# Another dealing of the modulation slabs over the first layer's projections, and another place for their requests

## The chip, the cores and the metric

The kernel runs on one core of a Trainium2 chip. The metric is the device time of one execution in microseconds. TensorE does the matrix products, VectorE (DVE) and ScalarE (ACT) the elementwise work, GpSimd (POOL) some set-up and a few transfers; SyncE (SP) asks for nearly all transfers from HBM, in one queue.

## The reference

A decoder of two layers on 256 tokens of width 2048, in float32. Cut to what matters:

```python
cs = silu(c)                                   # one vector of 2048
for l in range(2):
    mod = cs @ ada_w[l] + ada_b[l]             # six vectors of 2048
    sh_a, sc_a, g_a, sh_m, sc_m, g_m = split(mod, 6)
    h = x * (1 + sc_a) + sh_a
    if l == 0:
        y = gla_mixer(h, w_in, ...)            # q, k, v, r = h @ w_in; gated linear attention in 4 chunks;
                                               # o = rms_norm(o) * silu(r); o @ w_out
    else:
        k, v = split((x * (1 + sc_k) + sh_k) @ w_kv)   # sh_k, sc_k = cs @ kv_ada_w + kv_ada_b
        y = stick_breaking(h @ w_q, k, v) @ w_out
    x = layer_norm(alpha * x + (1 + g_a) * y)
    h = x * (1 + sc_m) + sh_m
    x = layer_norm(alpha * x + (1 + g_m) * (relu(h @ w1 + b1) ** 2 @ w2 + b2))
```

## The kernel before

**Tiles.** The weights of the large products come in tiles of 128 x 1024 float32 (0.52 MB), 768 in all, in a fixed order of stages: `lead` (k and q of layer 0), `gv` (v, 32 tiles), `gr` (r, 32), `go` (the output projection of layer 0, 32), `u0`, `d0` (its MLP, 128 each), then layer 1. A loop body is 16 tiles (`BODY`). Each tile goes through a ring of four buffers (`RING`): SP asks for it into `raw`; ScalarE rounds it to the upper half `w_hi` (L439); VectorE subtracts to get the lower half `w_lo` (L873); TensorE multiplies the tokens' two halves by `w_hi` (L1330, L1331) and the upper one by `w_lo` (L1334), four times each. `stripe_tile` and `wide` do this in the first layer. SP may ask for tile t once VectorE has done tile t-4, ScalarE may round it once TensorE has used tile t-4.

**Slabs.** The vectors `mod` are made beside that by VectorE. A slab is 128 x 2048 float32 (1.05 MB) of the transposed modulation weights; one `scalar_tensor_tensor` (L878, in `mod_tile`) multiplies it by `cs` and sums along the row, which gives 128 elements of `mod`. There are 224 slabs, 16 to a vector. The first 32 (the shift and scale of the first product) go through eight buffers in `lead`. The other 192 share the two buffers of `mod_w`; SP may ask for a slab once the slab two before it is done:

```python
def load_mod(a, slot, first=False):
    if not first:
        sp.wait_ge(mod_done, a - 1)
    sp.dma_start(mod_w[:, slot, :], mods[bass.ds(a, 1), :, :]...)
```

In this text slabs are counted from the first of these 192 (0, 1, ...). Slabs 0 and 1 are asked for and done at the end of `lead`.

**The order.** `SCHEDULE` says for each body how many slabs are dealt to it, and `MOD_AT` behind which tiles of a body they lie for each such number. VectorE works in `body` tile by tile: the lower half, the slabs dealt to that tile, then what else hangs on the tile as a hook. SP's `body` goes the same way: it asks for tile j and then for the slabs dealt to position j, and each request waits in the queue for its own release. `MODS_DONE` (VectorE) and `MODS_LOADED` (SP) override `MOD_AT` for single bodies; before, they do so for `gv`'s first body and for `go`'s second.

**Around the change.** In `gv` VectorE has more to do than halves and slabs: the gates' logarithm (L1099), their running sums (L1105, L1114), and the keys and queries with their decays (L1126 to L1144). The gates' product is TensorE's hook behind tile 1 of `gv` (L1578), the scores' product (80 small matmuls, L1589) the one behind tile 25; ScalarE copies the scores (L670) as a hook behind tile 28, VectorE masks them behind tile 30. In `gr` TensorE has the four heads' output (L1603), in `gr` and `go` the turning of o (L1464). The slabs of `gv` make the gate `g_a0`, which is read in `gr`; those up to `go`'s second body make `sh_m0` and `sc_m0`, which are read at the end of `go` (`make_coef`).

Of the kernel before, what the change touches and what calls it, by code (L numbers as in the profile page):

```python
# [35 lines left out]
T0 = {}  # L36
_at = 0
for _n, _s in _sizes:
# [14 lines left out]

MOD_AT = {12: (0, 1, 3, 4, 5, 7, 8, 9, 11, 12, 13, 15), 10: (1, 2, 4, 5, 7, 8, 10, 12, 13, 15), 8: tuple(range(1, 16, 2)), 6: (1, 4, 6, 9, 12, 14), 4: (0, 2, 5, 9), 2: (10, 14), 0: ()}

SCHEDULE = [("gv", 0, 1, 8), ("gv", 16, 1, 10), ("gr", 0, 1, 12), ("gr", 16, 1, 8), ("go", 0, 1, 8), ("go", 16, 1, 2), ("u0", 0, 1, 0), ("u0", 16, 7, 8),
            ("d0", 0, 4, 6), ("d0", 64, 1, 2), ("d0", 80, 2, 6), ("d0", 112, 1, 0), ("aq", 0, 1, 2), ("aq", 16, 1, 6), ("ak", 0, 2, 4),
            ("av", 0, 1, 4), ("av", 16, 1, 6), ("ao", 0, 1, 8), ("ao", 16, 1, 0), ("u1", 0, 1, 0), ("u1", 16, 4, 4), ("u1", 80, 10, 0), ("d1", 112, 1, 0)]
PLAN = {}
_a = LEAD  # L60
for _n, _off, _bodies, _per in SCHEDULE:
    for _b in range(_bodies):
# [40 lines left out]
def unsplit_before(t):  # L103

    return N_LEAD + early_before(t)
# [6 lines left out]
def build_kernel(nc, tiles, mods, c_t, x_rows, mod_b, ln_t, b1_t, w_gl, wgu, normg_t, ln_rows, b2_rows, out):  # L112
# [3 lines left out]
    with ctx:  # L116
# [136 lines left out]
            return (rows_buf, turned_buf)[tok][:, pr * SEQ:(pr + 1) * SEQ]  # L253

        GO_MODS = {6: (0,), 9: (1,)}
        MODS_DONE = {T0["gv"]: {1: (2,), 3: (3,), 4: (4,), 5: (5,), 10: (6,), 15: (7,)}, T0["go"] + 16: GO_MODS}
        MODS_LOADED = {T0["gv"]: {3: (2, 3), 4: (4,), 5: (5,), 10: (6,), 15: (7,)}, T0["go"] + 16: GO_MODS}

        def mod_positions(per_body):
            return {j: (i,) for i, j in enumerate(MOD_AT[per_body])}  # L260
# [14 lines left out]
        def _(sp):  # L275
# [11 lines left out]
# [3 lines that stand above are left out]
                sp.dma_start(mod_w[:, slot, :], mods[bass.ds(a, 1), :, :].rearrange("a p n -> p (a n)"))\  # L290
                  .then_inc(mod_loaded[slot], 16)
# [16 lines left out]
            def body(t, a, per_body, at=None, skipped=0, early=False, ahead=None, from_lead=False):  # L308
                at = at or mod_positions(per_body)
                for j in range(BODY):  # L310
                    if not early or j >= EARLY:
                        load_tile(t + j, j % RING, skipped=skipped, unsplit=from_lead and j < RING)
                    if ahead is not None and j in EARLY_LOAD:
                        load_early(ahead, EARLY_LOAD.index(j))
                    for i in at.get(j, ()):
                        load_mod(a + i, i % 2)
# [24 lines left out]
            for i in range(2):  # L341
                sp.wait_ge(mod_done, LEAD - LEAD_BUFS + i + 1)
                load_mod(LEAD + i, i, first=True)
            for name, off, bodies, per in SCHEDULE:
                t = T0[name] + off
# [3 lines left out]
                if bodies == 1:  # L349
                    body(t, PLAN[t][0], per, MODS_LOADED.get(t), skipped=unsplit_before(t), early=t in EARLY_AT, from_lead=t == N_LEAD,  # L350
                         ahead=EARLY_AT.index(t + BODY) if t + BODY in EARLY_AT else None)
# [508 lines left out]
        def _(dve):  # L860
# [32 lines left out]
            def body(t, a, lap, per, hooks, early=False, at=None):  # L893
                at = at or mod_positions(per)
                for j in range(BODY):
                    if not early or j >= EARLY:
                        split_tile(t + j, j % RING, ring_used=t if early and j < EARLY + RING else None)
                    for i in at.get(j, ()):
                        mod_tile(a + i, mod_w[:, i % 2, :], mod_loaded[i % 2], lap + i // 2 + 1)
                    for f in hooks.get(j, ()):  # L900
                        f()

            def run(t, hooks=None):
                a, per = PLAN[t]
                body(t, a, (a - LEAD) // 2, per, {j: H.get(t + j, []) for j in range(BODY)} if hooks is None else hooks, t in EARLY_AT,
                     MODS_DONE.get(t))

# [907 lines left out]
```

## Time and profile before

| | |
|---|---|
| time, three runs | 2262.27, 2263.2, 2265.02 us (median 2263.2) |
| the profiled execution | 2265.58 us, its span 2263.9 us |
| TensorE busy (matmul) | 2231.3 us, 99% of the span, granted clock 0.997 |
| VectorE busy | 1723.9 us, 76% |
| ScalarE busy | 1136.3 us, 50% |
| read from HBM | 655.22 MB, 290 GB/s over the span |

The span runs from the first to the last instruction; times of day in the rows count from its start. Busy shares are averages over stages with different limits: `lead` lasts to about 144 us, `gv` to 252, `gr` to 352, `go` to 432. TensorE's matmuls overlap in the records (one of 512 columns is listed with 0.39 us and the next starts 0.23 us later), so its own progress is read from the starts of rows.

### The profile page before, as it was taken

The numbers are of one execution on the slowest core, as the hardware profiler recorded it, in microseconds if no ns is written. First come the engines' busy times: TensorE is split into PE (matmuls) and PEld (weight loads), VectorE is DVE, ScalarE is ACT, GpSimd is POOL, SyncE is SP. The second block draws the span as 40 slices with busy tenths as digits, with TensorE's granted clock in tenths as the row PEclk, the third lists the DMA queues.
The fourth block names the chain that finished last, engine by engine and source line by source line (L and its number), as shares of the span: only waits on it lengthen the run. The fifth ranks groups of instructions, "written<-read, shape, count | busy, mean of one in ns | idle before, by whom it ended". The sixth has DMA issues, their size and how long they took to land.

```text
span 2263.9 us, 32088 instructions
## 1 busy us (share of the span) xinstructions
PE 2231.3 (99%) x10940; PEld 1870.6 (83%) x10940; DVE 1723.9 (76%) x1706; ACT 1136.3 (50%) x1408; POOL 19.0 (1%) x41
## 2 busy tenths in 40 slices
PE   8999999999999999999999999999999999999998
PEld 6786788788888888888888888888888888888886
DVE  6689889988888888898777867888766455556656
ACT  2144455565555554444555555545555555444443
POOL 1000000000000000000000000000000000000000
PEclk9999999999999999999999999999999999999999
DMA  9998999679999999969768766784877555755563
GB/s 393 417 375 316 359 385 383 228 288 375 375 383 376 380 366 351 341 241 355 283 224 325 270 237 237 313 313 144 305 287 267 186 193 203 253 194 193 191 208 125
DMA packets 146474, 658.60 MB, mean 291 GB/s; under 512 B 16496, under 2 KB 16816, under 8 KB 115792
## 3 DMA queue, kind: packets, MB, share of 16 engines
q1 hardware_dynamic: 144000, 642.05, 75.8%
q0 software_dynamic: 2384, 15.37, 1.7%
q8 instruction: 54, 0.88, 0.2%
q14 instruction: 36, 0.29, 0.0%
HBM read 655.22 MB, written 2.13 MB: 290 GB/s over the span
## 4 chain that ended last, share of the span: by engine, by line
PE 84%; DMA 7%; DVE 6%; issue 2%; ACT 1%; SPq 1%; DVEq 0%; ACTq 0%
PE ps L1432 20%; PE ps L1330 16%; PE ps L1334 16%; PE ps L1331 16%; PE ps L1434 10%; DMA R<-in_mods 3%; DMA mod_w<-in_mods 2%; DMA raw<-in_tiles 2%; DVE mod_w L878 1%; DVE w_lo L873 1%; DVE X L956 1%; DVE stats L958 1%; DVE S L953 1%; PE ps L1534 0%; PE ps L1532 0%
## 5 line engine op out<-in xcount | busy, mean ns | idle before, releaser
L873 DVE TENSOR_TENSOR w_lo<-raw,w_hi 128x1024 fp32r<-128x1024 f32 x720 | 876.9, 1222 | 447.1 <-ACT w_hi L439 443.0
L439 ACT ACTIVATE w_hi<-raw 128x1024 fp32r<-128x1024 f32 x720 | 760.0, 1059 | 833.3 <-PE ps L1334 365.7
L1330 PE MATMUL ps<-w_hi,h_both 128*128 128x512 f32 x1872 | 735.8, 393 | 3.3 <-ACT w_hi L439 3.3
L1331 PE MATMUL ps<-w_hi,h_both 128*128 128x512 f32 x1872 | 729.1, 389 | 0.0
L1432 PE MATMUL ps<-h_both,w_hi 128*128 128x512 f32 x1920 | 666.3, 394 | 0.0
L1434 PE MATMUL ps<-h_both,w_lo 128*128 128x256 f32 x1920 | 532.1, 277 | 0.0
L1334 PE MATMUL ps<-w_lo,h_both 128*128 128x512 f32 x1872 | 506.9, 390 | 2.1 <-DVE w_lo L873 1.9
L878 DVE SCALAR_TENSOR_TENSOR mod_w<-mod_w,cs 128x2048 f32<-128x2048 f32 x200 | 456.9, 2285 | 30.7 <-DMA mod_w<-in_mods 22.2
L1432 PEld LDWEIGHTS ps<-h_both,w_hi 128*128 128x128 f32 x1920 | 360.0, 188 | 83.8
L1330 PEld LDWEIGHTS ps<-w_hi,h_both 128*128 128x128 f32 x1872 | 351.6, 188 | 78.9 <-ACT w_hi L439 3.7
L1334 PEld LDWEIGHTS ps<-w_lo,h_both 128*128 128x128 f32 x1872 | 350.6, 188 | 79.2 <-DVE w_lo L873 6.2
L1331 PEld LDWEIGHTS ps<-w_hi,h_both 128*128 128x128 f32 x1872 | 351.6, 188 | 72.2 <-issue 1.0
L1434 PEld LDWEIGHTS ps<-h_both,w_lo 128*128 128x128 f32 x1920 | 360.4, 188 | 0.1
L1210 DVE TENSOR_TENSOR h_both<-R,h_both 128x512 fp32r<-128x512 f32 x128 | 87.5, 684 | 2.9 <-ACT h_both L763 2.9
L763 ACT ACTIVATE h_both<-R 128x512 fp32r (+1 forms) x128 | 78.6, 614 | 0.0
L1344 PE MATMUL ps<-R,raw 128*128 128x256 f32 x256 | 56.7, 381 | 2.8 <-ACT R L624 1.4
L1344 PE MATMUL ps<-R,odd_raw 128*128 128x256 f32 x256 | 57.0, 381 | 2.2 <-ACT R L624 2.2
L1344 PEld LDWEIGHTS ps<-R,raw 128*128 128x128 f32 x256 | 48.1, 190 | 11.1 <-ACT R L624 3.0
L1344 PEld LDWEIGHTS ps<-R,odd_raw 128*128 128x128 f32 x256 | 48.1, 190 | 10.9 <-ACT R L624 4.6
L624 ACT ACTIVATE R<-R,coef 128x256 f32<-128x256 f32 x16 | 9.6, 600 | 93.2 <-DVE coef L1079 93.2
L878 DVE SCALAR_TENSOR_TENSOR R<-R,cs 128x2048 f32<-128x2048 f32 x16 | 36.7, 2292 | 19.1 <-DMA R<-in_mods 19.1
L499 ACT ACTIVATE S<-ps,b1t 128x256 f32<-128x256 f32 x120 | 46.6, 471 | 0.0
(195 smaller groups left out, 1037.6 us busy)
## 6 DMA issues: line engine op xcount, KB each, us to landing
raw<-in_tiles SPq DMA_DIRECT2D x736, 512.0 KB, 4.8
mod_w<-in_mods SPq DMA_DIRECT2D x200, 1024.0 KB, 7.1
R<-in_mods SPq DMA_DIRECT2D x16, 1024.0 KB, 21.9
odd_raw<-in_tiles SPq DMA_DIRECT2D x16, 512.0 KB, 20.3
R<-in_tiles SPq DMA_DIRECT2D x16, 512.0 KB, 6.3
R<-in_ln_rows POOLq DMA_DIRECT2D x6, 1024.0 KB, 8.3
G<-in_mods SPq DMA_DIRECT2D x4, 1024.0 KB, 22.0
S<-in_mods SPq DMA_DIRECT2D x4, 1024.0 KB, 24.0
```

Of the source, the lines that this page charges most:

```text
L439: nc.scalar.activation(w_hi[:, slot, :], raw[:, slot, :], ACT.Copy).then_inc(hi_ready, 1)
L499: ins = nc.scalar.activation(turned_buf[:, blk * SEQ:(blk + 1) * SEQ], ps[:, 4 * par + blk, SEQ:2 * SEQ], ACT.Identity, bias=b1t[:, bass.d ...
L763: nc.scalar.activation(h_hi[:, slot:slot + 2, :], R[:, bass.ds(kt * SEQ, 2 * SEQ)].rearrange("p (a t) -> p a t", a=2), ACT.Copy).then_inc( ...
L873: nc.vector.tensor_tensor(w_lo[:, slot, :], raw[:, slot, :], w_hi[:, slot, :].bitcast(F32), ALU.subtract)\
L878: nc.vector.scalar_tensor_tensor(buf, buf, 1.0, cs[:], ALU.mult, ALU.mult, accum_out=mod_t[:, bass.ds(a, 1)]).then_inc(mod_done, 1)
L1210: nc.vector.tensor_tensor(h_lo[:, slot:slot + 2, :], R[:, bass.ds(kt * SEQ, 2 * SEQ)].rearrange("p (a t) -> p a t", a=2), h_hi[:, slot:slo ...
L1330: mm(dst, h_hi[:, kt, toks], w_hi[:, slot, c], start=start, stop=False, skip_group_check=more)
L1331: return mm(dst, h_lo[:, kt, toks], w_hi[:, slot, c], start=False, stop=False, skip_group_check=more)
L1334: return mm(dst, h_hi[:, kt, tok * P:(tok + 1) * P], w_lo[:, slot, c], start=False, stop=stop, skip_group_check=more)
L1344: last = mm(ps[:, 2 * (2 * half + k) + blk // 2, (blk % 2) * SEQ:(blk % 2 + 1) * SEQ], w[:, k * SW + blk * P:k * SW + (blk + 1) * P], xT[: ...
L1432: mm(ps[:, bank, :], w_hi[:, j % RING, c], h_both[:, kt, :, :].rearrange("p a t -> p (a t)"), start=kt == 0, stop=False, skip_group_check= ...
L1434: last = mm(ps[:, bank, 0:SEQ], w_lo[:, j % RING, c], h_hi[:, kt, :], start=False, stop=kt == KT - 1, skip_group_check=True)
```

## The change

The number of slabs dealt to `gv`'s two bodies becomes 6 and 12 instead of 8 and 10; `gr` keeps 12 and 8. The order on VectorE is written out for both bodies of `gv` (`MODS_DONE`), and the places of SP's requests for both bodies of `gv` and of `gr` (`MODS_LOADED`). A request then stands at the position four tiles behind the one at which VectorE does the slab two before. So the requests for the last two slabs of `gv` stand in `gr` (entries -2 and -1). From `go` on nothing is changed.

```diff
-SCHEDULE = [("gv", 0, 1, 8), ("gv", 16, 1, 10), ("gr", 0, 1, 12), ("gr", 16, 1, 8), ("go", 0, 1, 8), ("go", 16, 1, 2), ("u0", 0, 1, 0), ("u0", 16, 7, 8),
+SCHEDULE = [("gv", 0, 1, 6), ("gv", 16, 1, 12), ("gr", 0, 1, 12), ("gr", 16, 1, 8), ("go", 0, 1, 8), ("go", 16, 1, 2), ("u0", 0, 1, 0), ("u0", 16, 7, 8),
...
         GO_MODS = {6: (0,), 9: (1,)}
-        MODS_DONE = {T0["gv"]: {1: (2,), 3: (3,), 4: (4,), 5: (5,), 10: (6,), 15: (7,)}, T0["go"] + 16: GO_MODS}
-        MODS_LOADED = {T0["gv"]: {3: (2, 3), 4: (4,), 5: (5,), 10: (6,), 15: (7,)}, T0["go"] + 16: GO_MODS}
+        MODS_DONE = {T0["gv"]: {1: (2,), 3: (3,), 4: (4,), 10: (5,)},
+                     T0["gv"] + 16: {2: (0,), 4: (1,), 7: (2,), 8: (3,), 9: (4,), 10: (5, 6), 11: (7,), 12: (8,), 13: (9,), 14: (10,), 15: (11,)},
+                     T0["go"] + 16: GO_MODS}
+        MODS_LOADED = {T0["gv"]: {3: (2, 3), 5: (4,), 7: (5,), 8: (6,), 14: (7,)},
+                       T0["gv"] + 16: {6: (2,), 8: (3,), 11: (4,), 12: (5,), 13: (6,), 14: (7, 8), 15: (9,)},
+                       T0["gr"]: {0: (-2,), 1: (-1,), 2: (0,), 3: (1,), 4: (2,), 5: (3,), 7: (4,), 8: (5,), 9: (6,), 11: (7,), 12: (8,), 13: (9,), 15: (10,)},
+                       T0["gr"] + 16: {0: (-1,), 1: (0,), 3: (1,), 5: (2,), 7: (3,), 9: (4,), 11: (5,), 13: (6,), 15: (7,)},
+                       T0["go"] + 16: GO_MODS}
```

## Rows read from the trace of the kernel before

**Rows 1.** The page: TensorE's busy time, share and instructions.

```profile
PE 2231.3 (99%) x10940; PEld 1870.6 (83%) x10940; DVE 1723.9 (76%) x1706; ACT 1136.3 (50%) x1408; POOL 19.0 (1%) x41
```

**Rows 2.** Busy time by stretch, from `gv` on; last three columns clock, DMA share, GB/s.

```profile
144.00:206.00 62.00, 59.74 (x263) 47.41 (x261) 57.79 (x62) 32.37 (x30) 1.97 (x2) 1.00 0.79 302
206.00:248.00 42.00, 39.14 (x206) 31.20 (x205) 34.95 (x34) 14.12 (x14) 0.00 (x0) 1.00 0.87 337
248.00:306.00 58.00, 58.00 (x236) 43.86 (x235) 46.45 (x43) 32.56 (x53) 0.51 (x1) 1.00 0.99 385
306.00:352.00 46.00, 46.00 (x214) 38.08 (x213) 41.30 (x38) 23.25 (x31) 0.56 (x1) 1.00 0.99 377
352.00:398.00 46.00, 46.00 (x210) 38.03 (x210) 40.84 (x39) 24.07 (x30) 1.05 (x2) 1.00 1.00 397
432.00:2263.90 1831.90, 1819.25 (x9095) 1536.17 (x9093) 1374.15 (x1341) 957.86 (x1183) 7.37 (x14) 1.00 0.74 272
```

**Rows 3.** Timeline of TensorE: lower-half products of tiles 0, 2, 3, 25, 26, 34, 64.

```profile
146.47 1.07 PE L1334 MATMUL ps<-w_lo,h_both 128*128 128x512 f32 x4
...
152.89 1.07 PE L1334 MATMUL ps<-w_lo,h_both 128*128 128x512 f32 x4
155.61 1.07 PE L1334 MATMUL ps<-w_lo,h_both 128*128 128x512 f32 x4
...
223.86 1.07 PE L1334 MATMUL ps<-w_lo,h_both 128*128 128x512 f32 x4
...
236.38 1.08 PE L1334 MATMUL ps<-w_lo,h_both 128*128 128x512 f32 x4
...
258.15 1.07 PE L1334 MATMUL ps<-w_lo,h_both 128*128 128x512 f32 x4
...
352.73 1.07 PE L1334 MATMUL ps<-w_lo,h_both 128*128 128x512 f32 x4
```

**Rows 4.** TensorE's waits from 144 to 252 us: total, times, longest.

```profile
PE ps L1330 <- ACT w_hi L439: 3.3, 4, 1.1
PE ps L1334 <- DVE w_lo L873: 1.7, 5, 0.4
```

**Rows 5.** Timeline of VectorE: start, duration, work, and the idle time before it.

```profile
156.34 1.22 DVE L873 TENSOR_TENSOR w_lo<-raw,w_hi 128x1024 fp32r<-128x1024 f32 x1
...
205.97 2.28 DVE L878 SCALAR_TENSOR_TENSOR mod_w<-mod_w,cs 128x2048 f32<-128x2048 f32 x1
...
208.18 1.22 DVE L873 TENSOR_TENSOR w_lo<-raw,w_hi 128x1024 fp32r<-128x1024 f32 x1
...
215.73 2.29 DVE L878 SCALAR_TENSOR_TENSOR mod_w<-mod_w,cs 128x2048 f32<-128x2048 f32 x1 [1.85 <-DMA mod_w<-in_mods]
...
236.25 1.22 DVE L873 TENSOR_TENSOR w_lo<-raw,w_hi 128x1024 fp32r<-128x1024 f32 x1 [4.10 <-ACT w_hi L439]
...
252.80 1.23 DVE L873 TENSOR_TENSOR w_lo<-raw,w_hi 128x1024 fp32r<-128x1024 f32 x1
...
350.87 2.35 DVE L873 TENSOR_TENSOR w_lo<-raw,w_hi 128x1024 fp32r<-128x1024 f32 x2
```

**Rows 6.** VectorE's waits from 156 to 208 us.

```profile
DVE w_lo L873 <- ACT w_hi L439: 1.3, 2, 0.9
DVE R L1099 <- ACT R L649: 0.6, 1, 0.6
DVE mod_w L878 <- DMA mod_w<-in_mods: 0.4, 1, 0.4
```

**Rows 7.** Timeline of SP's queue: requests for slabs (L290) and tiles (L284).

```profile
208.29 0.33 SPq L290 DMA_DIRECT2D mod_w<-in_mods  x1
...
258.12 0.33 SPq L290 DMA_DIRECT2D mod_w<-in_mods  x1
258.49 0.91 SPq L284 DMA_DIRECT2D raw<-in_tiles  x2
```

**Rows 8.** The slabs' requests (L290) between 200 and 306 us, 21 of them.

```profile
DMA to landing us min/median/max: 4.8/6.9/9.1
```

## The prediction, made before the changed kernel ran

> **What bounds the kernel now.** I read the page first: TensorE is busy for 2231.3 of 2263.9 us [rows 1]. So no change of order can bring more than some 30 us, and an edit matters only where TensorE stands still or is paced by others. The stretches of the trace then show where that is [rows 2]: from 248 us to the end of the first half of `go` it is busy in every microsecond, in `gv` it is not.
>
> The size of the hole comes from TensorE's own rows [rows 3]. Number the tiles from `gv`'s first (0); `gr` begins at 32, `go` at 64. An undisturbed tile takes 2.72 us (tile 2 to tile 3, 152.89 to 155.61). From tile 0's lower part (146.47) to tile 34's (258.15) are 111.68 us. 34 tiles need 92.48. The gates' matrix product takes 152.89 - 146.47 - 2 x 2.72 = 0.98, the scores behind tile 25 take 236.38 - 223.86 - 2.72 = 9.80. So **8.4 us** are lost, all before tile 26. The waits of TensorE in this stretch name both feeders [rows 4]: the upper halves from ScalarE and the lower halves from VectorE, 5.0 us together (the rest is the slow start of the matmuls after each wait).
>
> Who is late behind them? VectorE's rows give its prices [rows 5]: a slab holds it for 2.21 us (205.97 to the lower half at 208.18; the rows' own durations overlap by 0.08), a lower half for 1.14, its 1.22 less that overlap. From 156.34 (tile 5) to 208.18 it does 16 lower halves (18.2 us), slabs 5 to 10 (13.3), waits 2.3 us [rows 6], and the remaining 18.0 us are the gates, keys and queries. It is the bound there, at 96%. From 206 us on it is the reverse: it waits on slabs (215.73) and 4.10 us for ScalarE (236.25), which stands in the copy of the scores [rows 5]. The transfers moved 302 GB/s up to 206 us, 337 to 248, then 385, 377 and 397 at a share of 0.99 to 1.00 [rows 2]. So TensorE is in front of a hard-working VectorE first and of full transfers later.
>
> **The change, part by part.** No instruction is added or removed: the same slabs, the same tiles, the same arithmetic. Two things move.
>
> *Slabs on VectorE.* In the old order slabs 5, 6, 7 lie behind tiles 5, 10, 15 and 8 to 17 behind 17 to 31. In the new one slab 5 is behind 10, slabs 6 and 7 behind 18 and 20, and 8 to 17 behind 23, 24, 25, 26, 26, 27, 28, 29, 30, 31. Up to slab 8's end VectorE has, from 156.34: 19 lower halves (21.7), slabs 5 to 8 (8.8), the same 18.0, and about 1.2 of waits (half of the old 2.3, since the upper half of tile 6 is asked for earlier). That makes 206.0. The lower half of tile 25 follows one half and one slab later, ending at 210.5; TensorE without holes wants it at 223.86 - 8.4 = 215.4. The same sum at the tight places leaves 3 us at tile 8 and some 1.5 us at tile 14. So I take the whole 8.4 us as regained by tile 25. While TensorE does the scores (9.8 us), VectorE has slabs 11 to 14 to do, which it could not reach in the old order before it stood for 4.10 us.
>
> *Requests on SP's queue.* SP asks for tile k once VectorE is done with tile k-4, and for slab i once slab i-2 is done. The old order in `gr`'s first half puts slab i where it is used. One case [rows 7]: tile 34's lower half starts at 252.80 and ends at 254.0, which frees tile 38's buffer; SP stands at a slab until 258.12 and asks for two tiles only at 258.49, 4.5 us late. In the new order a slab's request stands four tiles behind slab i-2's use, so the release that SP waits for comes right behind the one for the tile. What is queued behind it, the next tile, is no longer held; the slabs' own requests are as early as before. SP's issue costs of 0.33 to 0.43 us are the same in number. But each slab now has one more tile ahead of it in the same queue.
>
> *What it costs later.* The 8.4 us are kept only if slabs and tiles come that much sooner in `gr`. There are two slab buffers, so a slab in a row of slabs costs (2.29 + landing)/2. The landings between 200 and 306 us are 4.8 at the least, 6.9 in the median and 9.1 at most [rows 8]: 3.55, 4.6 and 5.7 us a slab. From the other side, one slab and one tile are 1.57 MB, which at the 397 GB/s of the fullest stretch [rows 2] take 3.96 us. I take 4.0: the burst has one tile to a slab, where the old trace has more tiles than slabs in flight, so the landing should lie below the median.
>
> Slab 10 is asked for at 206.0 and lands 7.4 us later, as slab 12 did in the old trace at the same traffic (asked for at 208.29 [rows 7], used at 215.73 [rows 5]): 213.4. Slab 19, behind tile 33, starts nine slabs later, at 249.4; it and tile 34's lower half end 3.4 us on, at 252.8. TensorE without holes wants that half at 258.15 - 8.4 = 249.7. So 3.1 us are given back there, and 5.3 kept. With 3.55 us a slab nothing is given back; with 4.6, all but 0.1.
>
> *Behind that.* At tile 64 VectorE's lower half ends at 352.1 (350.87 is two of them), and TensorE takes it at 352.73: 0.6 us in hand [rows 3, 5]. TensorE now comes 5.3 us sooner, so the stream must be 4.7 us sooner. From 206 to 398 us it moves 42 x 337 + 58 x 385 + 46 x 377 + 46 x 397 = 72.1 MB [rows 2] in 192 us. If the idle share of the 42 us goes, and all runs at the middle of the three full rates, 385, this takes 187.2 us, 4.8 less; at 377 it is 0.8 less, at 397 it is 10.4 less. With the 0.6 in hand: 1.4, 5.4 and 8.4 kept (the last capped by the hole). I take another 0.3 off the 5.3 for such pinches: **5.0 us**. From 432 us on TensorE is its own bound, busy for 1819 of 1832 us [rows 2], so what is kept goes through to the end; gate and coefficient columns use the same slabs with the same deadlines from `go` on.
>
> The profiled execution took 2265.6 us (span 2263.9). Minus 5.0 it would be 2260.6; the median of the runs is 2.4 lower, 2263.2, and gives **2258.2**.
>
> One page speaks against it. The Trainium skill, "DMA: Bandwidth & Descriptors", section "Specifications" (and "Where 436 GB/s comes from"), puts what one core gets from HBM at about 358 GB/s and says that this side binds. By it, 72.1 MB take 201 us, no stream could be pressed together, and the sum would be 0. The trace does not agree: it shows 385 over 58 us and 397 over 46.
>
> **The rivals.**
> - *Full gain* (the hole is closed, nothing given back): 8.4 us, 2254.8. For it: 397 GB/s was held for 46 us; later tile requests are up to 4.5 us earlier. Against: it needs under 3.7 us a slab, which is 1.57 MB at 425 GB/s, more than any of rows 2.
> - *Mostly given back in `gr`*: the transfers are the bound, at 377 to 385 GB/s, and a slab costs 4.3 to 4.5. Kept are 1 to 3.5 us, 2261.
> - *Nothing changes*: VectorE's burst at 4.6 us a slab gives back all that `gv` gains; within 1 us, 2263.2. The row for it is the median landing. The page's 358 GB/s would lead here too.
> - *Slower*: the burst of 10 slabs behind 9 tiles makes tile 34 late by more than 8.4 us. It decides from 4.6 us a slab, that is a landing of 6.9 us, and each further microsecond of landing costs 4.5. With 7.4, as slab 12 had, it is 4.85 us a slab, tile 34's half at 260.4, TensorE 10.7 late: 2.3 us slower than before, 2265.5. For it: the median is at the edge. Against: with fewer tiles in flight beside a slab it should land sooner.
>
> **How the numbers follow.** Forecast (kept 3.5 to 6.5 us) 0.45, full gain (6.5 and more) 0.18, mostly given back 0.17, nothing 0.10, slower 0.10. 0.2% of this kernel is 4.5 us. Two thirds of the forecast's case lie beyond it: faster 0.30 + 0.18 = 0.48. Slower by that much is half of the last case, 0.05. The same: 0.47. The range runs from the full gain, 2254.8, to 0.7 us below the old time, 2262.5; outside are the slower case, half of "nothing" and a little below. The likeliest case alone is 2256.7 to 2259.7.
>
> **What would show it.** Tile pitch 2.72 us from tile 2 to 25, the scores starting near 216.5 instead of 224.9; the 4.10 us wait of VectorE gone, with slab waits in its place around 210 to 250; SP asking for tiles in `gr`'s first half within 0.5 us of their release; TensorE with 2 to 4 us of waits on lower halves between tiles 31 and 39, where it had none; transfers over 390 GB/s between 206 and 306. Wrong would make it: upper halves late in `gr` since raw tiles queue behind slabs, a slab cost away from 4.0, or a pinch at tile 64 that eats more than 0.3.

## The result, and the profile after

The change made the kernel slower. Its median is 2266.96 us (2263.59 to 2270.01, 22 runs) against 2264.06 us (2262.16 to 2269.23, 22 runs) for the kernel before, a ratio of 1.0013, with a 95% interval of 1.0008 to 1.0019 (such intervals stand in square brackets from here on). Some 2.9 us are lost, where 5.0 were forecast as gained. 2266.96 lies outside the range of 2254.8 to 2262.5. The profiled execution of the new kernel took 2268.2 us with a span of 2266.4 us, 2.5 more than the span before.

In the new kernel the lines stand six further down: the upper half is rounded at L445, the lower one made at L879, a slab done at L884, and TensorE's product of the lower half is L1340. The page of the profile shows the same work as [rows 1], in a longer span:

```profile
PE 2231.5 (98%) x10940; PEld 1874.2 (83%) x10940; DVE 1722.7 (76%) x1706; ACT 1138.3 (50%) x1408; POOL 19.1 (1%) x41
```

TensorE's timeline, which answers to [rows 3], shows where the time went. These are its lower-half products of tiles 2, 3, 25, 26, 31, 32, 34, 38 and 64, one upper product that follows tile 31, and the upper product at the head of tile 54:

```profile
152.85 1.07 PE L1340 MATMUL ps<-w_lo,h_both 128*128 128x512 f32 x4
155.57 1.07 PE L1340 MATMUL ps<-w_lo,h_both 128*128 128x512 f32 x4
...
215.41 1.07 PE L1340 MATMUL ps<-w_lo,h_both 128*128 128x512 f32 x4
...
227.93 1.08 PE L1340 MATMUL ps<-w_lo,h_both 128*128 128x512 f32 x4
...
246.42 2.08 PE L1340 MATMUL ps<-w_lo,h_both 128*128 128x512 f32 x4 [3.90 <-DVE w_lo L879]
248.29 0.63 PE L1336 MATMUL ps<-w_hi,h_both 128*128 128x512 f32 x1
...
250.85 1.07 PE L1340 MATMUL ps<-w_lo,h_both 128*128 128x512 f32 x4
...
257.73 1.19 PE L1340 MATMUL ps<-w_lo,h_both 128*128 128x512 f32 x4 [1.28 <-DVE w_lo L879]
...
272.30 1.21 PE L1340 MATMUL ps<-w_lo,h_both 128*128 128x512 f32 x4 [0.79 <-DVE w_lo L879]
...
323.08 0.50 PE L1336 MATMUL ps<-w_hi,h_both 128*128 128x512 f32 x1 [0.44 <-ACT w_hi L445]
...
355.11 1.17 PE L1340 MATMUL ps<-w_lo,h_both 128*128 128x512 f32 x4
```

Read against [rows 3]: at tile 25 the new kernel is 223.86 - 215.41 = 8.45 us ahead, and at tile 26, behind the scores, still 8.45. The hole in `gv` is closed whole. At tile 34 it is ahead by 258.15 - 257.73 = 0.42 us: eight microseconds are gone within eight tiles. At tile 64 it is 355.11 - 352.73 = 2.4 us behind, and that is what arrives at the end. So there are two losses, 8.0 us between tiles 26 and 34 and 2.8 us between 34 and 64. The second is over before tile 64: TensorE's rows put it at tiles 35 to 39 (1.2 us), 46 and 47 (0.4) and 54 and 55 (1.2), and at tile 55 (328.16, before 325.82) it is already 2.3 us behind.

TensorE's waits name nearly one feeder alone, VectorE. First those between 144 and 252 us, where [rows 4] had 5.0 us spread over nine waits, then those from 252 to 432 us, where the kernel before had none:

```profile
PE ps L1340 <- DVE w_lo L879: 4.4, 2, 3.9
...
PE ps L1340 <- DVE w_lo L879: 2.1, 2, 1.3
PE ps L1336 <- ACT w_hi L445: 0.4, 1, 0.4
```

Why VectorE was late stands in its own timeline. The rows are slab 10, slab 16, the lower half of tile 31, slab 17, slab 19, and, a hundred microseconds later, the half of tile 64:

```profile
214.24 2.29 DVE L884 SCALAR_TENSOR_TENSOR mod_w<-mod_w,cs 128x2048 f32<-128x2048 f32 x1 [2.50 <-DMA mod_w<-in_mods]
...
241.61 2.29 DVE L884 SCALAR_TENSOR_TENSOR mod_w<-mod_w,cs 128x2048 f32<-128x2048 f32 x1 [2.19 <-DMA mod_w<-in_mods]
...
245.16 1.21 DVE L879 TENSOR_TENSOR w_lo<-raw,w_hi 128x1024 fp32r<-128x1024 f32 x1
246.29 2.28 DVE L884 SCALAR_TENSOR_TENSOR mod_w<-mod_w,cs 128x2048 f32<-128x2048 f32 x1
...
254.24 2.29 DVE L884 SCALAR_TENSOR_TENSOR mod_w<-mod_w,cs 128x2048 f32<-128x2048 f32 x1 [1.18 <-DMA mod_w<-in_mods]
...
353.82 1.22 DVE L879 TENSOR_TENSOR w_lo<-raw,w_hi 128x1024 fp32r<-128x1024 f32 x1
```

From slab 10 to slab 19, nine slabs on, are 254.24 - 214.24 = 40.0 us, 4.44 us a slab. The half of tile 31 ends at 246.37, and TensorE starts on it at 246.42. Its upper half was there twelve microseconds earlier, by ScalarE's row:

```profile
233.36 1.06 ACT L445 ACTIVATE w_hi<-raw 128x1024 fp32r<-128x1024 f32 x1 [3.19 <-DMA raw<-in_tiles]
```

So TensorE did not lack the tile. The lower half stood in VectorE's fixed order behind slab 16, and slab 16 had not landed. The masking of the scores, which stands between the two on VectorE (243.83 to 245.16), held it for another 1.3 us.

The windows show what the transfers did meanwhile, by the stretches of [rows 2]; the last three columns are the granted clock, the DMA share and GB/s:

```profile
206.00:248.00 42.00, 37.60 (x199) 30.59 (x198) 31.63 (x31) 12.13 (x13) 0.00 (x0) 0.98 0.91 346
248.00:306.00 58.00, 55.87 (x219) 41.01 (x218) 46.47 (x44) 31.11 (x52) 0.51 (x1) 0.98 0.97 355
306.00:352.00 46.00, 45.43 (x207) 36.90 (x206) 40.22 (x37) 24.05 (x30) 0.56 (x1) 1.00 1.00 395
352.00:398.00 46.00, 46.00 (x212) 37.91 (x211) 42.72 (x41) 23.36 (x29) 1.05 (x2) 1.00 0.99 390
```

In 6 us slices the burst looks like this (TensorE's busy time is the first number behind the comma):

```profile
218.00:224.00 6.00, 6.00 (x52) 5.21 (x52) 2.66 (x3) 0.00 (x0) 0.00 (x0) 1.00 0.96 357
224.00:230.00 6.00, 6.00 (x37) 5.04 (x35) 5.66 (x6) 2.45 (x3) 0.00 (x0) 1.00 0.65 244
...
236.00:242.00 6.00, 5.50 (x25) 4.21 (x24) 3.81 (x4) 1.06 (x1) 0.00 (x0) 1.00 0.95 359
242.00:248.00 6.00, 2.10 (x7) 1.38 (x6) 6.00 (x8) 1.99 (x2) 0.00 (x0) 0.87 0.84 315
248.00:254.00 6.00, 6.00 (x24) 4.89 (x23) 5.06 (x6) 2.21 (x3) 0.00 (x0) 0.85 0.94 339
```

The transfers are not the wall: VectorE waits for a slab again and again while they move 244 to 359 GB/s. They are short of requests. SP's queue (L290 tiles, L296 slabs) shows it:

```profile
217.71 0.33 SPq L290 DMA_DIRECT2D raw<-in_tiles  x1
220.29 5.97 SPq L296 DMA_DIRECT2D mod_w<-in_mods  x2
227.07 0.38 SPq L290 DMA_DIRECT2D raw<-in_tiles  x1
...
257.71 1.46 SPq L290 DMA_DIRECT2D raw<-in_tiles  x2
```

Between 217.71 and 227.07 no tile is asked for, since no lower half is done in that time: VectorE does slabs 11 and 12 and waits for them. A slab is asked for as soon as the one two before it is done, as meant, and yet the ten slabs asked for between 206 and 250 us took, from request to landing:

```profile
DMA to landing us min/median/max: 5.6/7.0/7.5
```

### The profile page after: what moved, and what is told of

Its sections match the earlier page's. It is cut to its first block, busy times and chain, and to the rows that moved or that the text cites. A ratio compares the mean times of both kernels' runs of the same rounds, so it can differ in the third digit from the quotient of the medians.

```text
span 2266.4 us, 32088 instructions
## 1 busy us (share of the span) xinstructions
PE 2231.5 (98%) x10940; PEld 1874.2 (83%) x10940; DVE 1722.7 (76%) x1706; ACT 1138.3 (50%) x1408; POOL 19.1 (1%) x41
## 4 chain that ended last, share of the span: by engine, by line
PE 83%; DMA 9%; DVE 5%; issue 2%; SPq 0%; ACT 0%; DVEq 0%
PE ps L1438 19%; PE ps L1340 16%; PE ps L1336 16%; PE ps L1337 16%; PE ps L1440 10%; DMA mod_w<-in_mods 4%; DMA R<-in_mods 3%; DVE w_lo L879 1%; DMA S<-in_mods 1%; DVE mod_w L884 1%; DMA raw<-in_tiles 1%; DVE X L962 1%; DVE stats L964 1%; PE ps L1470 1%; DVE S L959 0%
## 5 line engine op out<-in xcount | busy, mean ns | idle before, releaser
L879 DVE TENSOR_TENSOR w_lo<-raw,w_hi 128x1024 fp32r<-128x1024 f32 x720 | 876.7, 1223 | 439.0 <-ACT w_hi L445 436.0
L445 ACT ACTIVATE w_hi<-raw 128x1024 fp32r<-128x1024 f32 x720 | 761.3, 1060 | 834.6 <-PE ps L1340 376.2
L1340 PE MATMUL ps<-w_lo,h_both 128*128 128x512 f32 x1872 | 507.7, 390 | 6.9 <-DVE w_lo L879 6.6
L884 DVE SCALAR_TENSOR_TENSOR mod_w<-mod_w,cs 128x2048 f32<-128x2048 f32 x200 | 457.1, 2286 | 42.1 <-DMA mod_w<-in_mods 33.9
L1340 PEld LDWEIGHTS ps<-w_lo,h_both 128*128 128x128 f32 x1872 | 351.2, 188 | 83.9 <-DVE w_lo L879 10.9
L884 DVE SCALAR_TENSOR_TENSOR R<-R,cs 128x2048 f32<-128x2048 f32 x16 | 36.7, 2293 | 19.5 <-DMA R<-in_mods 19.5
```

Of the source, the lines that this page charges most:

```text
L445: nc.scalar.activation(w_hi[:, slot, :], raw[:, slot, :], ACT.Copy).then_inc(hi_ready, 1)
L879: nc.vector.tensor_tensor(w_lo[:, slot, :], raw[:, slot, :], w_hi[:, slot, :].bitcast(F32), ALU.subtract)\
L884: nc.vector.scalar_tensor_tensor(buf, buf, 1.0, cs[:], ALU.mult, ALU.mult, accum_out=mod_t[:, bass.ds(a, 1)]).then_inc(mod_done, 1)
L1340: return mm(dst, h_hi[:, kt, tok * P:(tok + 1) * P], w_lo[:, slot, c], start=False, stop=stop, skip_group_check=more)
```

## The experiments

Two theories stood after this reading.

- *Round trip* (mine): two slab buffers, and a landing that does not fall below some 6 to 7 us even when the transfers have room, set 4.4 us or more a slab. The halves, and through them the next tiles' requests, queue behind the late slabs on VectorE. What would help is more slabs in flight or a shorter landing.
- *Requests*: the new places of the requests do the harm, since each slab now has a tile more ahead of it in SP's queue. What would help is the old places.

**The deal alone.** The new order on VectorE, each request where its slab is used:

```diff
-        MODS_LOADED = {T0["gv"]: {3: (2, 3), 5: (4,), 7: (5,), 8: (6,), 14: (7,)},
...
+        MODS_LOADED = {T0["gv"]: {3: (2, 3), 4: (4,), 10: (5,)},
+                       T0["gv"] + 16: {2: (0,), 4: (1,), 7: (2,), 8: (3,), 9: (4,), 10: (5, 6), 11: (7,), 12: (8,), 13: (9,), 14: (10,), 15: (11,)},
...
```

> The new dealing of slabs (6, 12, 12, 8), but every request at the position where its slab is used, as in the kernel before. Round-trip theory (a burst of slabs through two buffers costs VectorE 2.29 us plus a landing of 7 us for every two): the burst is the same, so the hole at tiles 30 to 34 is there and the time is within 1.5 us of the changed kernel, 2266 to 2268 beside a kernel before of 2264. Queue theory (the slabs' requests now stand behind more tiles and so land later): the landings are shorter, the gain of gv is kept, 2260 to 2262.

Measured: 2268.93 us (2266.59 to 2272.15), 1.0023 [1.0014, 1.0032], 0.9 us above what I expected from the round trip. It is the slowest of all, by its median 2 us slower than with the requests moved, though the two intervals touch. TensorE's row of tile 64 says the same (356.50 against 355.11). So the requests are not the harm, and rather a help. Slab 10 starts at 212.88, slab 19 at 255.00: 4.68 us each. TensorE's waits, 144 to 252 us and then 252 to 432, show what the moved requests had cured, the upper halves:

```profile
PE ps L1336 <- ACT w_hi L445: 3.0, 2, 2.5
PE ps L1340 <- DVE w_lo L879: 0.3, 1, 0.3
...
PE ps L1336 <- ACT w_hi L445: 4.6, 2, 2.5
```

**The requests alone.** The old deal (eight, ten, twelve, eight) with the requests four tiles behind the slab two ahead:

```diff
-SCHEDULE = [("gv", 0, 1, 6), ("gv", 16, 1, 12), ...
+SCHEDULE = [("gv", 0, 1, 8), ("gv", 16, 1, 10), ...
...
+        MODS_LOADED = {T0["gv"]: {3: (2, 3), 5: (4,), 7: (5,), 8: (6,), 9: (7,), 14: (8,)},
+                       T0["gv"] + 16: {3: (1,), 5: (2,), 6: (3,), 8: (4,), 9: (5,), 11: (6,), 12: (7,), 14: (8,)},
...
```

> The old dealing (8, 10, 12, 8) with the requests four tiles behind the use of the slab two before. Round-trip theory: the hole of gv stays, as VectorE's order is the old one, nothing new behind it: within 1.5 us of the kernel before. Queue theory: slab landings grow, TensorE waits in gr as it does in the changed kernel: 2 to 4 us slower than before.

Measured: 2264.41 us (2263.87 to 2266.02), 1.0000 [0.9991, 1.0009]. The hole in `gv` stays, with these waits up to 252 us and none behind it:

```profile
PE ps L1340 <- DVE w_lo L879: 4.8, 8, 2.0
PE ps L1336 <- ACT w_hi L445: 0.7, 1, 0.7
```

So the requests alone lose 0.1 us, which is noise, the deal alone 4.6, both together 2.9. The theory of the requests falls.

**A third slab buffer.** The new kernel, with the tile `G`, idle until the gates need it, as a third buffer for slabs 10 to 27; each of these is asked for once the slab *three* before it is done (slab 10, the first in `G`, once `G` is idle), and its place in SP's order is moved to match:

```diff
+        MOD_BUFS = [mod_w[:, 0, :], mod_w[:, 1, :], G[:]]
+        def mod_place(n):
+            """buffer, lap and the slab before it in that buffer, for slab n after the lead"""
+            if not 10 <= n < 28:
+                return n % 2, n // 2 + 1 - (3 if n >= 28 else 0), n - 2
+            k = n - 10
+            return (2, 0, 1)[k % 3], k // 3 + (1 if k % 3 == 0 else 6), n - 3 if k else None
...
+                    sp.wait_ge(mod_done, LEAD + before + 1)
+                sp.dma_start(MOD_BUFS[slot], mods[a, :, :]).then_inc(mod_loaded[slot], 16)
...
+                    if occ == 0:
+                        act.wait_ge(mod_done, LEAD + 26)
```

> The changed kernel with a third slab buffer (G, which is free from the queries to the gate's row) for slabs 10 to 27, each asked for four tiles behind the use of the slab three before. The same bytes, the same VectorE order. Round-trip theory: (2.29 + 7) / 3 = 3.1 us a slab, below the 3.9 that one slab and one tile take on the transfers, so tile 34's lower half is in time or at most 3 us late: 2258 to 2262. Bandwidth theory (transfers are full from 206 us on, another buffer only lengthens the queue): landing grows to 10 us, the hole stays, 2266 to 2268.

Measured: **2256.46 us** (2256.29 to 2256.62, 6 runs), 0.9967 [0.9955, 0.9979]: 7.9 us faster than before, 10.5 faster than the change, and 1.5 below the least that I expected. TensorE has no wait left between 144 and 432 us. Slabs 10 and 19 on VectorE, and TensorE's product of tile 34:

```profile
212.37 2.29 DVE L906 SCALAR_TENSOR_TENSOR G<-G,cs 128x2048 f32<-128x2048 f32 x1
...
244.49 2.28 DVE L906 SCALAR_TENSOR_TENSOR G<-G,cs 128x2048 f32<-128x2048 f32 x1
```

```profile
249.68 1.07 PE L1366 MATMUL ps<-w_lo,h_both 128*128 128x512 f32 x4
```

That is 32.12 / 9 = 3.57 us a slab, and tile 34 at 258.15 - 249.68 = 8.47 us sooner than before: the whole hole is kept. The windows show full transfers in just the stretches where the change had 346 and 355 GB/s:

```profile
206.00:248.00 42.00, 42.00 (x224) 34.92 (x223) 40.47 (x40) 14.02 (x14) 0.00 (x0) 1.00 1.00 403
248.00:306.00 58.00, 58.00 (x236) 43.85 (x235) 51.72 (x46) 33.82 (x54) 1.06 (x2) 1.00 1.00 401
```

And the landing did not get shorter for it. The twelve slabs asked for between 206 and 250 us:

```profile
DMA to landing us min/median/max: 7.2/7.9/8.7
```

The slab costs less because three are on their way, not because one travels faster. The formula's (2.29 + 7.9)/3 = 3.4 is no longer the whole bound here: a slab and a lower half together are 2.21 + 1.14 = 3.35 us of VectorE's own work, and VectorE waited for slabs only 1.5 us in the whole burst. The start of slab 10, 1.9 us sooner than in the change, does not explain the gain: the run with an earlier start below has 3.9 us of that and loses them again.

**The old deal with the third buffer.** The edit above on the kernel before, its deal of eight and ten, requests ahead as well. It asks whether the buffer alone is worth anything.

> The third slab buffer with the old dealing (8, 10, 12, 8). Round-trip theory: the hole of 8.4 us in gv is VectorE's own load before 206 us and stays to about 6 us or more; in gr TensorE had no waits, so there is nothing to win: 2261 to 2264.5. If the buffer alone were what brings the time, whatever the dealing: 2256 to 2258.

Measured: 2263.86 us (2262.52 to 2264.81) against 2263.85, 1.0001 [0.9992, 1.001]. Most of the hole in `gv` stands and nothing waits behind it. In the profiled execution tile 34's product is at 256.59, 1.6 us sooner than before, but the medians are the same. The waits up to 252 us are

```profile
PE ps L1366 <- DVE w_lo L901: 2.5, 7, 0.5
PE ps L1362 <- ACT w_hi L465: 0.7, 1, 0.7
```

So neither the deal nor the buffer is worth anything alone, and together, with the requests moved, they are worth 7.9 us: the deal closes the hole, the buffer pays for the burst that the deal makes.

**Half the bytes.** The new kernel, but slabs 10 to 19 transfer only their first 1024 columns. VectorE's instructions stay, so they read old data in the other half, and this part of `mod` is not computed.

```diff
-                sp.dma_start(mod_w[:, slot, :], mods[bass.ds(a, 1), :, :].rearrange("a p n -> p (a n)"))\
+                cols = slice(0, D // 2) if isinstance(a, int) and 10 <= a - LEAD < 20 else slice(0, D)
+                sp.dma_start(mod_w[:, slot, cols], mods[bass.ds(a, 1), :, cols].rearrange("a p n -> p (a n)"))\
```

> The changed kernel, in which the transfers of slabs 10 to 19 bring only the first half of the columns (the other half holds what was there, so that part of the modulation is not computed rightly); VectorE's work is the same. Round-trip theory: a landing is shorter by the 1.3 us that half a slab takes, so 3.9 us a slab in place of 4.4, slab 19 starts at 249 to 250, the hole at tiles 30 to 34 falls from 8.1 us to 2 to 4: 2260 to 2263. If VectorE's own work set the pace of the burst: no change, 2266 to 2268.

Measured: 2260.41 us (2257.3 to 2261.43), 0.9981 [0.9972, 0.999]. Slabs 10 and 19, and the landing of the slabs asked for between 206 and 250 us:

```profile
212.57 2.29 DVE L885 SCALAR_TENSOR_TENSOR mod_w<-mod_w,cs 128x2048 f32<-128x2048 f32 x1 [1.04 <-DMA mod_w<-in_mods]
...
247.43 2.29 DVE L885 SCALAR_TENSOR_TENSOR mod_w<-mod_w,cs 128x2048 f32<-128x2048 f32 x1 [0.86 <-DMA mod_w<-in_mods]
```

```profile
DMA to landing us min/median/max: 3.8/5.3/7.3
```

Half the bytes took a quarter off the median landing (7.0 to 5.3), and a slab costs 3.87 us: (2.29 + 5.3)/2 = 3.8. Two buffers with a shorter landing keep most of the hole too. That is the round trip's formula met a second time, from its other term. Taken alone this run would also fit a bound by bytes; the third buffer, with all the bytes, rules that out.

**An earlier start.** Slabs 6 to 11 behind tiles 16, 19, 21, 23, 24, 25 instead of 18, 20, 23, 24, 25, 26:

```diff
-                     T0["gv"] + 16: {2: (0,), 4: (1,), 7: (2,), 8: (3,), 9: (4,), 10: (5, 6), 11: (7,), ...
+                     T0["gv"] + 16: {0: (0,), 3: (1,), 5: (2,), 7: (3,), 8: (4,), 9: (5,), 10: (6,), 11: (7,), ...
```

> The changed kernel with slabs 6 to 11 dealt one to two tiles sooner (behind 16, 19, 21, 23, 24, 25 in place of 18, 20, 23, 24, 25, 26), into the 2 to 5 us that VectorE has in hand there. Round-trip theory: slab 10 is used near 211 us and not at 214.2, every later slab of the burst 3 us sooner, so TensorE's hole at tiles 30 to 34 shrinks by 3 us and the half clock behind it may go too: 3 to 5 us faster than the changed kernel, 2262 to 2264. Queue theory: no change but for noise, 2266 to 2268.

Measured: 2266.45 us (2260.73 to 2268.59), 1.0007 [0.9998, 1.0017], which misses what I expected. Slab 10 starts 3.9 us sooner, and slab 19 only 1.2:

```profile
210.35 2.29 DVE L884 SCALAR_TENSOR_TENSOR mod_w<-mod_w,cs 128x2048 f32<-128x2048 f32 x1 [0.94 <-DMA mod_w<-in_mods]
...
253.06 2.29 DVE L884 SCALAR_TENSOR_TENSOR mod_w<-mod_w,cs 128x2048 f32<-128x2048 f32 x1 [1.59 <-DMA mod_w<-in_mods]
```

A slab cost 4.75 us here, at a median landing of 7.2: (2.29 + 7.2)/2 = 4.75. I had carried the 4.44 over as a constant; it moves with the landing. A head start is eaten by it: TensorE is 1.6 us ahead at tile 34 (256.55) and 0.8 behind at tile 38 (272.42), where it waits 1.9 us for a lower half.

**An even spread.** Two buffers, and slabs 11 to 45 dealt out one to each 4.84 us over `gv`'s end, `gr` and `go`'s first half, in place of the burst (`MODS_DONE` and `MODS_LOADED` of five bodies).

> The changed kernel with its two buffers, but slabs 11 to 45 dealt evenly over TensorE's time, one each 4.84 us, from tile 25 to tile 79; requests still four tiles behind the use of the slab two before. Round-trip theory: two buffers can give a slab each 4.4 to 4.8 us, so the lower halves are no longer behind a burst; TensorE keeps most of the 8.4 us of gv and loses 0 to 4 in small waits: 2257 to 2262. If the burst is not the matter but the slabs still owed after tile 25 (two more than before): waits turn up later and add up to the same, 2265 to 2267.

Measured: 2263.93 us (2261.49 to 2268.0), 1.0001 [0.9992, 1.001]: 3 us better than the change, no better than before, between the two expectations. There is no wait of TensorE before 252 us; from 252 to 432 it has

```profile
PE ps L1344 <- DVE w_lo L883: 4.4, 3, 2.8
```

The 8.4 us were moved to another place, tiles 54 to 81, but not kept. There the transfers are full: 398 GB/s from 352 to 398 us, after 346 and 375 GB/s from 206 to 306. So the last wait reads as one for bytes that two buffers had not fetched earlier. No other spread was tried.

## Why the prediction was wrong, point by point

**The hole: right.** 8.4 us were read from [rows 3], and 8.45 were regained, with a pitch of 2.72 us at every tile up to 25. VectorE was the bound there, and moving slabs 5, 6 and 7 to later tiles lifted it.

**SP's queue: right.** Tiles are asked for as their buffer comes free: tile 34's half is done at 257.7, and tile 38's request stands at 257.71, where it was 4.5 us late before [rows 7]. The deal alone, slower by some 2 us, suggests that this was worth something once the burst was there.

**The failed step: "I take 4.0" us a slab.** The formula, (2.29 + landing)/2, was the right one, to 0.2 us. With the median landing of the burst it gives 4.65, and 4.44 was measured (the landings run down to 5.6). For the earlier start it gives 4.75 (4.75 measured), for half the bytes 3.8 (3.87). Of its three landings I took neither the median nor the maximum but argued that with fewer tiles in flight "the landing should lie below the median". It did not: 7.0 us against the 6.9 of [rows 8], at 346 GB/s. The slab cost 4.44 us. The nine slabs cost 4.0 us more than forecast and slab 10 started 0.8 later (214.24, not 213.4: its request stood at 207.29 and not 206.0, and it landed after 7.0 us and not 7.4). With the 3.1 us already in the sum that is 7.9 given back at tile 34, where 8.0 were measured. Of the 4.9 us that the sum lacked there, 4.0 are this one term.

The value of 3.96, "from the other side", from 1.57 MB at 397 GB/s, was a floor and not a second estimate. It holds only if enough requests stand in the queue to fill the transfers, and two buffers do not see to that. The run with three buffers had them (403 GB/s) and even went below it, to 3.57 us, since 9 slabs go with 8 tiles there and some had landed ahead; the change did not come near. I let a bandwidth bound pull down a latency estimate.

**The reserve of 0.3 us behind tile 34: too small and in the wrong place, the second term.** I looked for a pinch at tile 64 alone and put 0.3 us on such pinches; 2.8 us were lost between tiles 34 and 55, and none to speak of at 64. My sum assumed that the stream would catch up by itself, at 377 to 397 GB/s from 206 us on. It moved 346 and 355 GB/s up to 306 us. VectorE's row of slab 19 in the kernel before is

```profile
250.44 2.29 DVE L878 SCALAR_TENSOR_TENSOR mod_w<-mod_w,cs 128x2048 f32<-128x2048 f32 x1 [0.46 <-DMA mod_w<-in_mods]
```

and in the new one it starts at 254.24, 3.8 us later; the lower half of tile 38 starts at 271.02 against 266.57, 4.5 us later. Before, TensorE took that half at 271.63, 3.8 us after its end, so what it had in hand there was less than the lateness, and in the new kernel it waits 0.79 us. At tile 54 it waits 0.44 us for an upper half whose tile had only just landed (ScalarE had waited 4.25 us for it). By tile 64 VectorE's half is still 2.9 us late (353.82 + 1.22 = 355.0 against 352.1 [rows 5]). The run with three buffers passes all these places without loss: tile 64 stands at 344.26, 8.47 us sooner than before, as tile 34 did. The run with half the bytes, whose slabs are whole again from slab 20 on, keeps more at tile 34 and then meets the second term as well. These are its tiles 34, 38 and 64,

```profile
250.92 1.20 PE L1341 MATMUL ps<-w_lo,h_both 128*128 128x512 f32 x4 [1.00 <-DVE w_lo L880]
...
265.50 1.20 PE L1341 MATMUL ps<-w_lo,h_both 128*128 128x512 f32 x4 [0.80 <-DVE w_lo L880]
...
346.73 1.08 PE L1341 MATMUL ps<-w_lo,h_both 128*128 128x512 f32 x4
```

7.2, 6.1 and 6.0 us sooner than before. Its median gives only 3.4 us (its profiled execution, 2258.7, is 1.7 below its median), so the sizes are those of one execution. That the second term comes from the same round trip is what these rows suggest; no run changes it alone.

**The rivals.** The time came out as in *slower*, at 0.10: 2266.96, where it had 2265.5. It named the place (tile 34) and the mechanism (the burst of slabs on VectorE). But its 4.6 us a slab were not reached. At tile 34 the new kernel still had 0.4 us, which is nearer to *nothing changes*, also at 0.10, whose row is the median landing of 6.9. What made it slower is the second term, which neither rival had. That *slower* comes nearest to the measured time is therefore in part luck. The median of the only row there was should have been the forecast, not two edges of it. *Mostly given back* had the right price, 4.3 to 4.5 us a slab, from the wrong cause: it took the transfers as the bound at 377 to 385 GB/s, by which a slab and a tile take 4.1 to 4.2 us and not 4.3 to 4.5, and they moved 346 and 355.

**The rule that spoke against the change.** By the Trainium skill, "DMA: Bandwidth & Descriptors" ("Where 436 GB/s comes from"), some 358 GB/s bind. The change's 346 and 355 GB/s seem to agree with it, and do not: with a third buffer the same stretches moved 403 and 401. A note under the measured table of the same page of the Trainium skill gives about 358 GB/s as each core's part when both cores of the pair stream. The Trainium skill, "Perfetto Trace Analysis" ("Roofline"), says that a core alone can pull more than this share, up to about 435. The 403 here lie within that.

## What to carry to other kernels

A stream behind N buffers costs about (use + landing)/N an item, where neither the bytes nor the consumer's own work cost more. With two buffers that was the price here within 0.2 us; with three the consumer's own work had nearly caught up with it. Take the landing from the median row of such requests and do not lower it because the transfers look idle: idle transfers (a share of 0.91 here) beside a consumer that waits are a sign that buffers, not bytes, are the bound. When work is moved out of a stretch into a burst elsewhere, count the buffers in flight there before the instructions, and follow how late the moved stream itself then is at every later place where the engine that matters has little in hand, not at one. Two edits that bring nothing alone can be the two halves of a gain.

## What I had not expected of the hardware

- A 1.05 MB slab took 5.6 to 7.5 us to land, median 7.0, in a stretch whose transfers were at 346 GB/s, and 7.2 to 8.7, median 7.9, in the run with three buffers, where they were at 403. Half of it took 5.3. So 14% less traffic went with a landing 11% shorter, too little to make up for the missing buffer.
- TensorE's 3.90 us wait cost more than itself. The granted clock is 0.87 and 0.85 in the two 6 us slices around 248 us, and the matmuls after it start 0.43 us apart (248.29, 248.72 and 249.14) instead of 0.23, the 1.2 GHz level instead of 2.4. Tile 32 took 250.85 - 246.42 = 4.43 us instead of 2.72. Here these 1.7 us were covered: TensorE waited 1.28 us for VectorE at tile 34 all the same.
